# Expert lists built by matrix products, the final root on ScalarE, and three moves around the start of the expert stage

## What is computed

```python
xp = xp + yp                                   # yp: merged branches @ w_out
xp = xp + hier_moe(rms_norm(xp, norm_ffn_g), ...)
y  = rms_norm(xp, norm_final_g)                # xf * rsqrt(mean(xf*xf) + EPS) * g

def hier_moe(h, w_rg, b_rg, w_re, b_re, w_g, w_u, w_d):
    # group = argmax of 4 group logits, then top 2 of the group's 8 expert logits
    # weights: softmax over the two, times the group's probability
    act = silu(h @ w_g[e]) * (h @ w_u[e])      # for each of 32 experts
    out = sum over e of (act * comb[:, :, e]) @ w_d[e]
```

## Time and profile before

| what | value |
|---|---|
| median of three runs | 1339.54 us |
| the profiled execution: time / span of its instructions | 1338.37 us / 1336.6 us |
| mean granted TensorE clock | 0.983 |
| busy: TensorE, its weight loads | 1264.2 us (95%), 1098.9 us |
| busy: VectorE, ScalarE, GpSimd | 928.5, 498.4, 481.5 us |
| DMA moved | 163.78 MB, mean 123 GB/s |

### The profile page before, as it was taken

One profiled execution on the slowest core, in us unless ns is written; L12 is line 12 of the kernel. 1 busy time (PEld: TensorE's weight loads), 2 busy tenths in 40 slices (PEclk: granted clock), 3 DMA queues, 4 the chain that ended last, 5 costly groups with the idle time before them and its releaser, 6 DMA issues.

```text
span 1336.6 us, 21305 instructions
## 1 busy us (share of the span) xinstructions
PE 1264.2 (95%) x7533; PEld 1098.9 (82%) x7533; DVE 928.5 (69%) x2190; ACT 498.4 (37%) x1074; POOL 481.5 (36%) x768
## 2 busy tenths in 40 slices
PE   5999999999989999998999998999999979999985
PEld 5999999999979999997777766999788758877742
DVE  5665888888899998854777775342656558777636
ACT  5554222122212113224665553000422237665533
POOL 5801595968884116643000010210012234333314
PEclk9999999999999999998999999999999989999998
DMA  7201232121213221103000231843222258999757
GB/s 258 72 27 42 78 85 81 37 79 38 70 36 123 96 67 56 28 1 100 1 16 2 67 100 50 297 149 135 111 96 79 79 203 301 348 341 342 298 196 317
DMA packets 79312, 163.78 MB, mean 123 GB/s; under 512 B 12529, under 2 KB 47937, under 8 KB 78065
## 3 DMA queue, kind: packets, MB, share of 16 engines
q1 hardware_dynamic: 65121, 129.31, 28.4%
q0 software_dynamic: 12656, 27.62, 6.1%
q10 hardware_dynamic: 1440, 5.58, 1.1%
HBM read 137.81 MB, written 39.21 MB: 132 GB/s over the span
## 4 chain that ended last, share of the span: by engine, by line
PE 78%; DMA 8%; POOL 5%; ACT 3%; DVE 3%; issue 2%; SPq 1%; POOLq 0%; ACTq 0%; DVEq 0%
PE bank L876 11%; PE bank L875 11%; PE bank L877 11%; PE bank L1085 4%; DMA region_h<-in_wd 4%; PE bank L1160 3%; PE bank L1267 3%; PE bank L1154 3%; PE bank L1003 2%; PE bank L1067 2%; PE bank L1172 2%; PE bank L1171 2%; PE bank L1173 2%; DMA region_t<-ffn_input_scratch,small_i 2%; PE bank L1156 2%
## 5 line engine op out<-in xcount | busy, mean ns | idle before, releaser
L1858 DVE MAX8 small<-region_kv 128x8 f32<-128x272 f32 (+4 forms) x241 | 190.2, 828 | 47.6 <-DVE region_kv L1863 47.5
L875 PE MATMUL bank<-h_hi,w_hi 128*128 128x384 f32 (+1 forms) x576 | 196.1, 340 | 0.0
L876 PE MATMUL bank<-h_lo,w_hi 128*128 128x384 f32 (+1 forms) x576 | 196.1, 340 | 0.0
L1863 DVE MATCH_REPLACE8 region_kv<-small,region_kv 128x272 f32<-128x272 f32 (+4 forms) x241 | 195.5, 818 | 0.0
L877 PE MATMUL bank<-h_hi,w_lo 128*128 128x384 f32 (+1 forms) x576 | 194.4, 338 | 0.0
L2189 POOL TENSOR_TENSOR w_lo<-w_stage,w_hi 128x512 fp32r<-128x512 f32 x64 | 80.8, 1299 | 144.8 <-ACT w_hi L1371 144.7
L875 PE MATMUL bank<-w_hi,h_hi 128*128 128x256 f32 x448 | 128.9, 288 | 2.3 <-ACT region_q L1434 2.3
L877 PE MATMUL bank<-w_hi,h_lo 128*128 128x256 f32 x448 | 125.9, 281 | 0.0
L876 PE MATMUL bank<-w_lo,h_hi 128*128 128x256 f32 x448 | 125.9, 281 | 0.0
L877 PEld LDWEIGHTS bank<-h_hi,w_lo 128*128 128x128 f32 x576 | 108.7, 189 | 0.0
L876 PEld LDWEIGHTS bank<-h_lo,w_hi 128*128 128x128 f32 x576 | 108.2, 188 | 0.6
(11 more groups left out here) (328 smaller groups left out, 3114.5 us busy)
## 6 DMA issues: line engine op xcount, KB each, us to landing
w_stage<-in_w_in SPq DMA_DIRECT2D x72, 256.0 KB, 3.2
region_kv<-in_xa SPq DMA_DIRECT2D x16, 512.0 KB, 5.8
region_q<-in_wg SPq DMA_DIRECT2D x12, 512.0 KB, 7.1
region_q<-in_wu SPq DMA_DIRECT2D x12, 512.0 KB, 19.4
region_q<-in_wd SPq DMA_DIRECT2D x12, 512.0 KB, 22.8
region_w<-in_wg SPq DMA_DIRECT2D x10, 512.0 KB, 7.1
region_w<-in_wu SPq DMA_DIRECT2D x10, 512.0 KB, 19.5
region_w<-in_wd SPq DMA_DIRECT2D x10, 512.0 KB, 22.6
```

Of the source, the lines that this page charges most:

```text
L875: mm(out, st_hi(k), mv_hi(k), start=(k == 0), stop=False)
L876: mm(out, st_hi(k), mv_lo(k), start=False, stop=False)
L1858: nc.vector.max(m8[:, q, :], x).then_inc(dve_c, 1)
L1863: nc.vector.match_replace(x, m8[:, q, :], x, TAKEN).then_inc(dve_c, 1)
```

## The change

Lists: `route` also multiplies the one-hot row of each choice by the pair (token code, weight) into `r_entry`, and `place` compares the rank with the numbers 0 to 127 into `r_at_place`; TensorE's new `listing(t)` sums the products of the two over all tiles in PSUM bank 2, so that the list heads arise on chip. The scatters to HBM stay (they serve the overflow pass); that of the last tile comes behind the first three gathers. The read-back (L835) is gone. The last tile's h2: GpSimd multiplies by the gain, ScalarE scales and issues the write. Experts 5 and 6 load after the first gather has landed. The overflow table comes behind `expert_lower(0)`, and nobody but SyncE waits for it at the start of the stage. `WARM` is 5. At the end ScalarE takes the root and VectorE the reciprocal; odd tiles are squared and scaled straight from PSUM. `entry_w` (the entries' weights for the scatter) is now filled by a copy from `pairs`.

```diff
-WARM = 14
+WARM = 5
@@ SyncE
             sp.wait_ge(a_oe, NG_ALL)
+            sp.dma_start(nflat[:, 576:740], a["consts"][:, K_END:K_ALL]).then_inc(g2_in, 16)
@@
-            for t in range(NT):
+            for t in range(NT - 1):
...
-                if t == NT - 1:
-                    sp.wait_ge(o7_done, 2 * NT)
-                    load_e(3)
...
-            sp.wait_ge(scattered, 16 * 2 * NT)
-            sp.dma_start(heads[:, :, :], lists[0:P, :, :]).then_inc(lidx_in, 16)
-            for e in range(4, NSLOT):
+            sp.wait_ge(o7_done, 2 * NT)
+            load_e(3)
+            sp.wait_ge(h2_last_out, 16)
+            load_e(4)
+            sp.wait_ge(hg_in[0], 16)
+            for e in range(5, NSLOT):
                 load_e(e)
@@ TensorE
+            def listing(t):
+                pe.wait_ge(list_ready, t + 1)
+                for q in range(2):
+                    last = mm(bank[2][:, 0:2 * NE], r_at_place[:, q, :], r_entry[:, t % 2, q, :], start=(t == 0 and q == 0),
+                              stop=(t == NT - 1 and q == 1), skip_group_check=True)
+                last.then_inc(listed, 1)
@@ out-projection loop, t = 1 .. 8
+                if t >= 3:
+                    listing(t - 3)
                 out_half(t, 0, 0, KD)
...
                 if t == NT - 1:
...
                     rank(t - 1)
+                    listing(t - 2)
...
             logits(NT - 1)
+            listing(NT - 2)
             rank(NT - 1)
+            listing(NT - 1)
             pe.wait_ge(pos_ready, NT)
@@
             pe.wait_ge(x2_ready, 2 * NT)
-            pe.wait_ge(over_ready, 1)
             e_trans(0)
@@ tail, odd tiles: the second column half first
-                    b, cs = bank[t - 1 + hf][:, :], slice(hf * 512, (hf + 1) * 512)
+                    b, cs = bank[t - hf][:, :], slice((1 - hf) * 512, (2 - hf) * 512)
@@ ScalarE, after the last norm2
+                    act.wait_ge(rstd_ready, NT)
+                    act.wait_ge(h2_scaled, 1)
+                    nc.scalar.activation(h2_last, h2_last, ACT.Copy, scale=tnrm[:, NT - 1, 1:2]).then_inc(h2_ready, 1)
+                    act.wait_ge(h2_ready, NT)
+                    act.dma_start(h2_d[(NT - 1) * P:NT * P, :], h2_last).then_inc(h2_last_out, 16)
                     route_exp(t - 1)
@@
             act.wait_ge(o7_done, 2 * NT)
-            act.wait_ge(over_ready, 1)
+            for s in range(2):
+                act.wait_ge(h2_out[s], 16 * (NT // 2))
@@ tail
+            nc.scalar.activation(froot[:, NT, :], eps_col, ACT.Sqrt)
...
+                    for hf in (1, 0):
+                        act.wait_ge(y1_pe, t + 1 - hf)
+                        nc.scalar.activation(fsq[:, t % 2, hf * 512:(hf + 1) * 512], bank[t - 1 + hf][:, :], ACT.Square,
+                                             scale=1.0 / 32.0, accum_out=fnrm[:, t, hf:hf + 1]).then_inc(fms_ready, 1)
...
+                            nc.scalar.activation(offset, offset, ACT.Identity, bias=eps_col).then_inc(fms_ready, 1)
...
+                nc.scalar.activation(froot[:, t, :], fnrm[:, t, 0:1], ACT.Sqrt, bias=offset).then_inc(frstd_ready, 1)
@@ VectorE, route
+                if t >= 2:
+                    dve.wait_ge(listed, t - 1)
+                for q in range(2):
+                    tt(r_entry[:, t % 2, q, :].rearrange("p (e w) -> p e w", w=2),
+                       r_oh[:, t, q * NE:(q + 1) * NE].unsqueeze(2).to_broadcast([P, NE, 2]),
+                       pairs[:, t, q, :].unsqueeze(1).to_broadcast([P, NE, 2]), ALU.mult)
@@ place
+                if t >= 1:
+                    dve.wait_ge(listed, t)
+                for q in range(2):
+                    last = ts(r_at_place[:, q, :], place_iota, r_rank[:, t, q:q + 1], None, ALU.is_equal)
+                last.then_inc(list_ready, 1)
+                nc.vector.tensor_copy(entry_w[:, t, :, 1], pairs[:, t, :, 1])
@@ after place(8)
-            h2_of(NT - 1)
-
-            dve.wait_ge(cnt_done, 1)
...
-            dve.wait_ge(lidx_in, 16)
+            dve.wait_ge(listed, NT)
+            found = bank[2][:, 0:2 * NE].rearrange("p (e w) -> p e w", w=2)
+            link(ts(heads[:, :, 0], found[:, :, 0], float(SENT), None, ALU.add))
             ts(gidx, heads[:, :, 0], 1, None, ALU.logical_shift_right).then_inc(gidx_ready, 1)
+            nc.vector.tensor_copy(pos_w[:, :, 1], found[:, :, 1])
...
             expert_lower(0)
+            overflow_table()
+            rows_lower(0)
             expert_lower(1)
-            rows_lower(0)
@@ final
+                link(nc.vector.reciprocal(froot[:, t, :], froot[:, t, :]))
...
+                for hf in range(2):
+                    cs = slice(hf * 512, (hf + 1) * 512)
+                    last = stt(out=x2[:, t, cs], in0=bank[t - 1 + hf][:, :], scalar=froot[:, t, :], in1=gfin[:, cs],
+                               op0=ALU.mult, op1=ALU.mult)
@@ GpSimd
+                if t == NT - 1:
+                    pool.wait_ge(x2_ready, 2 * NT)
+                    tt(h2_last, x2[:, t, :], gffn, ALU.mult).then_inc(h2_scaled, 1)
+                pool.wait_ge(ms_ready, t + 1)
+                rstd(tnrm, t).then_inc(rstd_ready, 1)
+            list_out(NT - 2)
@@
             for e in range(3):
                 gather(hg[:, e, :], gidx[:, e:e + 1], hg_in[e])
+            list_out(NT - 1)
...
-            for t in range(NT):
-                pool.wait_ge(fms_ready, t + 1)
-                rstd(fnrm, t).then_inc(frstd_ready, 1)
```

More of the change, by code:

```diff
@@ L68 @@
 K_END = K_THR + OVER_J
+K_ALL = K_END + P + 4 * NT
 def splits(n, most=512):
@@ L235, in build @@
         vjunk = sm(1)
+        eps_col = sm(1)
+        froot = sm(NT + 1, 1)
         pjunk = sm(3)
@@ L2028, in route @@
                 link(ts(r_den, r_ex, 1.0, r_gs, ALU.add, ALU.mult))
-                link(nc.vector.reciprocal(entry_w[:, t, 0, 1:2], r_den))
-                link(tt(entry_w[:, t, 1, 1:2], entry_w[:, t, 0, 1:2], r_ex, ALU.mult))
+                link(nc.vector.reciprocal(pairs[:, t, 0, 1:2], r_den))
+                link(tt(pairs[:, t, 1, 1:2], pairs[:, t, 0, 1:2], r_ex, ALU.mult))
+                if t >= 2:
[4 more added lines that the diff above has]
+                       pairs[:, t, q, :].unsqueeze(1).to_broadcast([P, NE, 2]), ALU.mult)
             def place(t):
@@ L2075, in _, with overflow_table @@
             place(NT - 1)
[L2076 to L2092 removed]
+            dve.wait_ge(listed, NT)
+            found = bank[2][:, 0:2 * NE].rearrange("p (e w) -> p e w", w=2)
+            link(ts(heads[:, :, 0], found[:, :, 0], float(SENT), None, ALU.add))
+            ts(gidx, heads[:, :, 0], 1, None, ALU.logical_shift_right).then_inc(gidx_ready, 1)
+            nc.vector.tensor_copy(pos_w[:, :, 1], found[:, :, 1])
+            def overflow_table():
+                dve.wait_ge(rank_done, NT + 1)
+                link(nc.vector.memset(f_one, 1.0))
+                link(nc.vector.tensor_copy(r_rb, bank[1][:, P:P + NE]))
+                link(tt(f_flag, r_rb.unsqueeze(1).to_broadcast([P, OVER_J, NE]),
+                        overthr.unsqueeze(2).to_broadcast([P, OVER_J, NE]), ALU.is_gt))
+                link(nc.vector.tensor_tensor_scan(f_cum, f_one, f_flag.rearrange("p a b -> p (a b)"), 0.0, ALU.mult, ALU.add))
+                link(ts(f_junk, f_cum, siota, 0.0, ALU.is_le, ALU.add, accum_out=f_id))
+                link(nc.vector.tensor_copy(over_i[:, 0:1], f_id))
+                nc.vector.tensor_copy(over_i[:, 1:2], f_cum[:, NE * OVER_J - 1:NE * OVER_J]).then_inc(over_ready, 1)
             def act_of(par):
@@ L2155, in final @@
                 dve.wait_ge(frstd_ready, t + 1)
-                stt(out=x2[:, t, :], in0=x2[:, t, :], scalar=fnrm[:, t, 1:2], in1=gfin,
-                    op0=ALU.mult, op1=ALU.mult).then_inc(fin_ready, 1)
+                link(nc.vector.reciprocal(froot[:, t, :], froot[:, t, :]))
+                if t % 2 == 0:
+                    stt(out=x2[:, t, :], in0=x2[:, t, :], scalar=froot[:, t, :], in1=gfin,
+                        op0=ALU.mult, op1=ALU.mult).then_inc(fin_ready, 1)
+                    return
+                for hf in range(2):
+                    cs = slice(hf * 512, (hf + 1) * 512)
+                    last = stt(out=x2[:, t, cs], in0=bank[t - 1 + hf][:, :], scalar=froot[:, t, :], in1=gfin[:, cs],
+                               op0=ALU.mult, op1=ALU.mult)
+                last.then_inc(fin_ready, 1)
             combine(0)
@@ L2180, in _ @@
             link(nc.gpsimd.memset(mhalf, -0.5))
+            link(nc.gpsimd.memset(eps_col, EPS))
             def split_lo(n):
@@ L2368, in _, with list_out @@
                 tt(wao_lo[c % 3][:, :, :], wao_raw[c % 3], wao_hi[c % 3][:, :, :].bitcast(F32), ALU.subtract).then_inc(wao_low, 1)
-            for t in range(NT + 2):
+            def list_out(t):
+                pool.wait_ge(pos_ready, t + 1)
+                for q in range(2):
+                    pool.indirect_dma_start(out=list_d, in_=entries[:, t, q, :], in_offset=None,
```

(14 more changed lines are left out.)

70 lines of the change are left out of this document (36 added, 34 removed).

## The result

The kernel after the change takes 1323.93 us (median of four runs, 1323.09 to 1326.4); beside them the kernel before took 1339.6 us (1336.98 to 1340.09). The ratio is 0.989, 95% interval 0.9871 to 0.9909. Measured twice more, on two chips, the same pair gave 0.9911 (0.9895 to 0.9927) and 0.9911 (0.9894 to 0.9927).

What follows compares the result with a forecast made beforehand. It took TensorE to bound the out-projection loop, a chain off TensorE the start, TensorE and DMA engines the expert stage. Terms -4.6 - 1.5 - 2.3 = -8.4 us gave 1331.0 us, range 1327.0 to 1336.5.

Steps and rivals of the forecast that it cites:

- Loop: Out-projection loop: seven listings on TensorE cost +3.3 us, VectorE's additions nothing.
- Start without the loop: Up to expert 0's matmuls: first transposes at 1085.6 for 1090.22, -4.6 us with the listings' cost included, clock -1.5 more.
- The clock: Expert 0's matmuls: without TensorE idling ahead of the transposes they run at the high clock, -1.5 us.
- Stage: Expert stage: an earlier start passes through to its end; expert 7's load priced at nothing, up to 2 us in range.
- Tail up to the last scaling: End of the kernel: root on ScalarE and squares from PSUM bring the last scaling to 1327.4, -2.7 us.
- rival C: End: Square and Sqrt share no table set, 18 loads cost 23 us on ScalarE; 1343.5 us, chance 0.07.
- The writes' cap: End: nine 512 KB writes behind the expert-row loads take until 1330.1, so the end gives -2.3 us.
- Behind the last landing: From the last write's landing to the end of the span: the prediction gave no term.
- Rival D: Start and end: gather and WARM both end sooner, the end gives its 2.8; -11 us, 1328.5, chance 0.10.
- A: Start: gather needs 7 us and expert 0 runs at low clock, or expert 7 comes late; -5.5, 1334, chance 0.20.
- B: Start: the first gather still takes 8.98 us, no clock gain; -3.4 us, 1336, chance 0.09.

Runs made afterwards that it cites:

- only_new_end: Kernel before the change with only the new tail (root on ScalarE, reciprocal on VectorE, odd tiles from PSUM); 1329.57 us, ratio 0.9953.
- old_end: Kernel after the change with the former tail (whole-row squares, copies out of PSUM, inverse root on GpSimd); 1331.14 us, ratio 0.9963.
- three_loads: Kernel after the change without SyncE's wait for the first gather, so nine weight loads are issued ahead of it; 1328.24 us, ratio 0.9945.
- after_again: Kernel after the change, unaltered, measured a second time; 1323.35 us, ratio 0.9911.
- after_third: Kernel after the change, unaltered, measured a third time; 1325.28 us, ratio 0.9911.
- table_first: Kernel after the change, but SyncE writes the overflow table before issuing the loads of experts 5 and 6; 1324.91 us, ratio 0.9911.
- warm14: Kernel after the change with WARM at its old 14 in place of 5; 1333.2 us, ratio 0.9979.
- hbm_lists: Kernel after the change with the lists read back from HBM and no listings on TensorE; 1327.93 us, ratio 0.9931.
- hbm_lists_warm10: Kernel after the change with the lists read back from HBM and WARM 10 in place of 5; 1324.86 us, ratio 0.9911.
- late_gpsimd_op: Kernel after the change with a one-column GpSimd memset behind the last root; 1328.06 us, ratio 0.9946.

## Why the prediction was wrong, by its own steps

**The sum, term by term.** With the means of the three profiles of after, and of before and only_new_end (start, stage) or before and old_end (tail, end):

- Loop: +3.3 forecast, +2.9 measured, 7 x 0.41. Right in kind; a listing costs a little less than the lower bound of 0.45, and VectorE's additions show no cost of their own.
- Start without the loop: -4.6 - 1.5 - 3.3 = -9.4 forecast, 21.82 - 31.95 = -10.1 measured. The row numbers came at 1078.6 (1079.1 forecast), the gather took 4.7 us (5.0), the warm-up 6.8 (7.1; its clock rose at about 1082.5, 4.6 us behind its start, where 5.4 were assumed): each step a little quicker, in the same order, and WARM did set the transposes.
- The clock, -1.5: right, and now shown. From the transposes to expert 1's first matmul it takes 8.17 us (before), 8.19 (only_new_end) and 8.11 (three_loads) where TensorE had idled 1.4 to 2.8 us ahead of them, and 6.65 (after), 6.69 (after_again) and 6.66 (after_third, table_first and warm14) where it hadn't. The window just behind expert 0's first matmuls shows a clock of 0.50 to 0.57 in the first group and of 1.00 in the second.
- Stage: 0 forecast, with up to 2 us for expert 7. Measured 187.0 - 185.9 = +1.1. Expert 7's load came 3.5 us late and not under 1 us, but with that gone (table_first) the stage stays within the profiles of after. The seven profiles with a start of 21.6 to 25.1 us have stages of 186.0 to 187.5 us (mean 186.7), the four with 26.4 to 32.4 and the same or the old lists 185.8 to 186.1. The place can be named: from expert 1 to expert 9 TensorE keeps one pace of about 5.6 us per expert in all thirteen profiles (expert 9's Silu starts 44.6 to 44.9 us behind expert 1's), and the profiles part from expert 10 on (expert 12's Silu is at 61.3 to 63.9 us). There TensorE begins to idle: in after it is busy for all 40.0 us from 1100 to 1140, and for 18.95 of the next 20 us, at a DMA share of 0.97. Part of an earlier start may be given back there; that is a guess, and after_again has 186.3 us, as much as before; why stays open, and so does why hbm_lists and hbm_lists_warm10 have 185 us.
- Tail up to the last scaling: -2.7 forecast, 41.97 - 44.48 = -2.5 measured. Right, and rival C falls: one table load, 1.28 us, at 1281.72, ahead of the loads of expert rows, none between squares and roots. The Trainium skill (ScalarE: Activation LUTs, "What ACT_TABLE_LOAD costs") has 2.66 us for a switch with its drain. The row has 1.28 for the load, and either is hidden here, as the loads of expert rows begin only at 1287.2.
- The writes' cap, which cut -2.7 to -2.3: half right. The last write was issued at 1321.4, right behind its scaling, and landed at 1324.2, 2.8 us later (before 2.6), so 0.2 of the 0.4 us came.
- **Behind the last landing: 0 forecast. From the last scaling to the end 4.49 - 7.74 = -3.25 us measured, from the last landing to the end 0.4 for 3.8.** This is the step that failed. The forecast followed the chain to the landing of the last write (1332.7) and gave what lies between it and the span's end (1336.6) no term and no reason, as if these 3.9 us were fixed. They were not: GpSimd's drain of 8.1 us ended them. The view of waits of before had it in plain sight, SyncE's 3.6 us in L80.

Together: 2.9 - 10.1 + 1.1 - 2.5 - 3.25 = -11.85 us, against 11.9 by the ratio of 0.9911. Without the last term it is -8.6, for -8.4 forecast; that this is so close is partly luck, since the start came out 0.7 us and the loop 0.4 us better and the stage 1.1 us worse than forecast. Rival D (more comes out) reached only to 1328.5, since it too stopped at the last landing. The missing term alone wouldn't have taken the time out of the range: 1339.54 - 11.9 = 1327.6 lies just inside it. It took the 3.8 us more by which the first medians differ as well. These 3.8 us aren't explained by any step; the intervals of the ratio overlap (0.9871 to 0.9909 for the first, 0.9895 to 0.9927 and 0.9894 to 0.9927 for the others). Rivals A and B fall with the gather's 4.7 us; A's late load of expert 7 came, later than A had it, and showed no cost.

**The weights within the sum.** The forecast named the lists as part of what brings the row numbers forward. True, and paid for in full in the loop. What carries the change is the shorter warm-up (7.65 us, warm14), which only pays because the first gather has three loads ahead of it and not nine (4.5 us, three_loads), and the end without GpSimd (6 to 7 us, only_new_end). The terms overlap, so they don't add. Two things are argued and not run: the shorter warm-up alone in the kernel before (there the gather landed 2.07 us behind the long one's end, so it should bring nothing), and the moves of the last h2 and of the overflow table to later places, which no run takes apart.

## What to carry to other kernels

Read the profile beyond the last write: if GpSimd's last useful instruction lies within some eight microseconds of the end, its closing drain (7.6 to 8.1 us here) may set the end, and moving that instruction to another engine gains more than its own time. A warm-up of TensorE is a bridge to the first data: measure when the data lands and end it there; too long costs its length (7.65 us for 18 matmuls more), too short costs the clock (1.5 us and more). And when a change has several parts, rebuild it without its largest part and re-tune the constant beside it, before crediting that part: without the lists on chip the ratio was 0.9931, and 0.9911, as with them, once WARM was re-tuned.

## What was not expected of the hardware

- GpSimd's closing DRAIN takes 7.6 us (7629 to 7638 ns, behind a memset) and 8.1 us (8144 ns twice, behind the inverse root). In late_gpsimd_op it takes its 7.6 us although the engine had idled 35.5 us and then run one memset of 0.1 us. TensorE's load queue drains for 6.3 to 7.9 us, VectorE 1.3, ScalarE 2.1 with the old tail and 0.33 with the new. Only the drain that ends last counts.
- A wait of the barrier is put down to PEq, whose drain had long ended; it was GpSimd.
- The overflow table's small write had landed 5.6 us behind its issue with no weights just ahead of it (table_first), 10.0 us behind it in three_loads and 12.1 us with six weight loads of 512 KB just ahead (after), each time by the issue of the read-back that waits for it.
